# A w_down product by seven block products, woven between those of gate and up

## What is computed

```
xn    = rms_norm(x, norm1)
proj  = xn @ w_in                                  # hyena x0, x1, v | q | k | v
mixed = concat(rms_norm(hyena(proj), hy_gain), rms_norm(window_attention(proj), at_gain))
h     = x + mixed @ w_out
gu    = rms_norm(h, norm2) @ w_gate_up             # 1024 -> 2 * 2816
gate, up = split(gu, 2)
y     = h + (silu(gate) * up) @ w_down             # 2816 -> 1024
```

## Time and profile before

| | us |
|---|---|
| median of 3 runs | 2817.58 (2816.18 to 2820.11) |
| the profiled execution | 2818.18 |
| its span, first to last instruction | 2816.4 |
| TensorE busy in the span | 2738.5 |
| VectorE / ScalarE / GpSimd busy | 1895.5 / 1226.2 / 1028.5 |
| w_down's matmuls, sum of listed durations | 938.7 (2376 of 512 columns) |
| mean granted TensorE clock | 0.991 |

### The profile page before, as it was taken

One profiled execution on the slowest core, in us unless ns is written; L12 is line 12 of the kernel. 1 busy time (PEld: TensorE's weight loads), 2 busy tenths in 40 slices (PEclk: granted clock), 3 DMA queues, 4 the chain that ended last, 5 costly groups with the idle time before them and its releaser, 6 DMA issues.

```text
span 2816.4 us, 38299 instructions
## 1 busy us (share of the span) xinstructions
PE 2738.5 (97%) x14266; PEld 2474.7 (88%) x14266; DVE 1895.5 (67%) x2612; ACT 1226.2 (44%) x1937; POOL 1028.5 (37%) x887
## 2 busy tenths in 40 slices
PE   8989999999998999999999999999999999999999
PEld 6877889888887888878999999999999989999998
DVE  6765676777577787767666666766665676566665
ACT  5564554444547777764232322422223333232321
POOL 1122121233212444464354543334454434343422
PEclk9999999999999999999999999999999999999999
DMA  6476997876897354454223221623322262222221
GB/s 218 146 260 197 300 257 231 282 211 183 230 256 204 111 150 131 121 164 142 86 87 94 86 87 59 244 65 98 94 89 91 72 221 81 65 72 65 71 70 66
DMA packets 388480, 405.30 MB, mean 144 GB/s; under 512 B 46270, under 2 KB 323390, under 8 KB 388007
## 3 DMA queue, kind: packets, MB, share of 16 engines
q1 hardware_dynamic: 358728, 322.50, 39.1%
q0 software_dynamic: 29568, 80.36, 8.9%
HBM read 292.14 MB, written 110.64 MB: 143 GB/s over the span
## 4 chain that ended last, share of the span: by engine, by line
PE 88%; DVE 4%; DMA 3%; ACT 2%; issue 2%; POOL 0%; SPq 0%; DVEq 0%; ACTq 0%; POOLq 0%
PE ff_banks L85 11%; PE ff_banks L87 11%; PE ff_banks L86 11%; PE ff_down L85 7%; PE ff_down L86 7%; PE ff_down L87 7%; PE pr_acc L85 4%; PE pr_acc L86 4%; PE pr_acc L87 4%; PE pr_gen L85 3%; PE pr_gen L87 3%; PE pr_gen L86 3%; PE am_mix L85 2%; PE am_mix L87 2%; PE am_mix L86 2%
## 5 line engine op out<-in xcount | busy, mean ns | idle before, releaser
L2802 POOL TENSOR_TENSOR ff_alo_raw<-ff_alo_raw,ff_silu 128x384 f32<-128x384 f32 x132 | 196.4, 1488 | 698.0 <-DVE ff_alo_raw L3025 624.4
L3047 DVE TENSOR_TENSOR ff_h<-ff_h,ff_down 128x512 f32<-128x512 f32 x396 | 265.1, 685 | 160.5 <-PE ff_down L87 157.4
L85 PE MATMUL ff_banks<-ff_xhi,ff_ghi 128*128 128x384 f32 x924 | 313.4, 339 | 6.3 <-DVE ff_glo L3035 3.8
L85 PE MATMUL ff_down<-ff_dhi,ff_ahi 128*128 128x512 f32 x792 | 313.0, 395 | 3.5 <-issue 3.5
L85 PE MATMUL pr_acc<-pr_xhi,pr_whi 128*128 128x386 f32 (+1 forms) x864 | 303.5, 351 | 11.4 <-DVE pr_xlo L1478 11.4
L86 PE MATMUL ff_down<-ff_dlo,ff_ahi 128*128 128x512 f32 x792 | 313.0, 395 | 0.0
L87 PE MATMUL ff_down<-ff_dhi,ff_alo 128*128 128x512 f32 x792 | 312.7, 395 | 0.0
L87 PE MATMUL ff_banks<-ff_xhi,ff_glo 128*128 128x384 f32 x924 | 312.1, 338 | 0.0
L86 PE MATMUL ff_banks<-ff_xlo,ff_uhi 128*128 128x384 f32 x924 | 311.0, 337 | 0.0
L85 PE MATMUL ff_banks<-ff_xhi,ff_uhi 128*128 128x384 f32 x924 | 310.7, 336 | 0.0
L86 PE MATMUL ff_banks<-ff_xlo,ff_ghi 128*128 128x384 f32 x924 | 310.5, 336 | 0.0
(11 more groups left out here) (308 smaller groups left out, 6518.5 us busy)
## 6 DMA issues: line engine op xcount, KB each, us to landing
ff_glo_raw<-w_gate_up SPq DMA_DIRECT2D x132, 256.0 KB, 3.2
ff_ulo_raw<-w_gate_up SPq DMA_DIRECT2D x132, 256.0 KB
ff_dlo_raw<-w_down SPq DMA_DIRECT2D x66, 512.0 KB, 4.4
pr_raw<-w_in SPq DMA_DIRECT2D x108, 256.0 KB, 6.5
f_dram<-fi_out POOLq DMA_DIRECT2D x32, 512.0 KB, 3.9
fs_a<-f_dram SPq DMA_DIRECT2D x32, 512.0 KB, 9.6
pr_xs<-x SPq DMA_DIRECT2D x18, 512.0 KB, 6.2
xkeep_dram<-pr_xs SPq DMA_DIRECT2D x18, 512.0 KB, 4.6
```

Of the source, the lines that this page charges most:

```text
L85: pe.matmul(out, still[0], moving[0], start=start, stop=False)
L2802: pool.tensor_tensor(block(prod, c), block(prod, c), silu[c][:], ALU.mult).then_inc(tempered, 1)
L3047: dve.tensor_tensor(h[j][:, o], h[j][:, o], down(v), ALU.add).then_inc(added, 1)
```

## The change

**In front.** Rows of w_down are loaded as 44 sets of four blocks of 128x128, one set for each of the first 44 events; GpSimd makes the four sums (or differences) of each set in four subtractions of 128 columns, and SP stores them to `dsum_dram`. Runs of 512 bytes, 256 KB in and 256 KB out for each set.

**In swiglu.** The product with w_down is made from seven block products as well: the activations of the step as 2x2 blocks (2 feature halves by 2 halves of 3 token tiles) with four sums made by GpSimd (`act_sums`), against w_down's blocks or their stored sums. Block product k is 3 triples (`lower(q, k)`), one for each token tile, 512 columns, and is added to its corner of h by three additions (`add(q, k)`). Some products accumulate on what an earlier one left in the bank, after it was read.

Gate and up: two PSUM banks X and Y in place of four. A chain stays open in its bank and is read between its products: ScalarE copies X after products 0, 2 and 4 (`keep`), VectorE adds Y to such a copy for C11, C12, C22, and C21 is read straight from X, by ScalarE's silu for gate and by VectorE's multiplication for up (`corner_straight`). So a product waits until the bank that it adds to was read.

The low and high parts of activations and w_down are made for each block product (`down_high`, `down_low`: 512 columns of w_down, then 384 of activations). The seven `lower(q - 1, k)` stand between the products of step q. The order on ScalarE, VectorE, GpSimd and SP is new. At a turn of group the low parts of T4 and B22 go to GpSimd. The rows h are loaded and the results stored by corners.

```diff
+        def bring_blocks(m):
+            if not 0 <= m < TP:
+                return
+            if m >= TB:
+                sp.wait_ge(t_out[(m - TB) % 2], 16 * ((m - TB) // 2 + 1))
+            n, o = m // 4, m % 4 * P
+            for i in range(2):
+                src = w_down[:, 2 * n + i, :].rearrange("p (h c) -> p h c", h=2)[:, :, o:o + P]
+                sp.dma_start(blocks[:, m % TB, 2 * i:2 * i + 2], src).then_inc(t_in[m % 2], 16)
+
+        def store_blocks(m):
+            if not 0 <= m < TP:
+                return
+            n, o = m // 4, m % 4 * P
+            sp.wait_ge(t_summed, 4 * m + 4)
+            sp.dma_start(dsum_dram[:, :, n, o:o + P].rearrange("x p c -> p x c"), blocks[:, m % TB]).then_inc(t_out[m % 2], 16)
+
         def second_half(rd, i, c):
...
+        def sum_blocks(m):
+            if not 0 <= m < TP:
+                return
+            b11, b12, b21, b22 = (blocks[:, m % TB, k] for k in range(4))
+            pool.wait_ge(t_in[m % 2], 32 * (m // 2 + 1))
+            pool.tensor_tensor(b11, b12, b11, ALU.subtract).then_inc(t_summed, 1)
+            pool.wait_ge(t_summed, 4 * m + 1)
+            pool.tensor_tensor(b12, b22, b12, ALU.subtract).then_inc(t_summed, 1)
+            pool.wait_ge(t_summed, 4 * m + 2)
+            pool.tensor_tensor(b22, b22, b11, ALU.subtract).then_inc(t_summed, 1)
+            pool.wait_ge(t_summed, 4 * m + 3)
+            pool.tensor_tensor(b21, b21, b22, ALU.subtract).then_inc(t_summed, 1)
+
         def evict(rd, i, c):
...
+    HT = WT // 2
     A11, A12, A22, S3, S1, S2, S4 = range(7)
     B11, B21, B22, T3, T1, T2, T4 = range(7)
-    STEPS = ((0, A11, B11), (1, S1, T1), (2, S2, T2), (3, A12, B21), (0, S3, T3), (2, A22, T4), (3, S4, B22))
+    X, Y = 0, 1
+    STEPS = ((X, A11, B11), (Y, A12, B21), (X, S2, T2), (Y, S1, T1), (X, S3, T3), (X, A22, T4), (Y, S4, B22))
...
+
+    NK = 7
+    STILL = (A11, A12, S2, S1, S3, A22, S4)
+    ADDED_TO = (C11, C11, C12, C22, C22, C21, C12)
+    LAST_ADDED = {C11: 1, C22: 4, C21: 5, C12: 6}
+    RAW_DOWN = {0: (0, 0), 1: (1, 0), 6: (1, 1)}
+    SUM_DOWN = {2: 3, 3: 0, 4: 1, 5: 2}
+    BEFORE_ON = {0: 5 - NK, 1: 6 - NK, 2: 0, 3: 1, 4: 2, 5: 4, 6: 3}
...
+        def bring_d(q, k):
...
+            if n >= DR:
+                sp.wait_ge(lowered, n - DR + 1)
+            f = 2 * (q % NC)
+            if k in RAW_DOWN:
+                row, half = RAW_DOWN[k]
+                src = w_down[:, f + row, 512 * half:512 * half + 512]
+            else:
+                src = dsum_dram[SUM_DOWN[k], :, q % NC, :]
+            sp.dma_start(din[n % DR][:], src).then_inc(d_in[n % DR], 16)
+
...
+        def act_sums(q, part):
...
+                pool.tensor_tensor(acts[:, S1], acts[:, S3], acts[:, A22], ALU.add).then_inc(a_summed, 1)
...
+                pool.tensor_tensor(acts[:, S2], acts[:, S1], acts[:, A11], ALU.subtract).then_inc(a_summed, 1)
...
+                pool.tensor_tensor(acts[:, S3], acts[:, A11], acts[:, S3], ALU.subtract).then_inc(a_summed, 1)
...
+                pool.tensor_tensor(acts[:, S4], acts[:, A12], acts[:, S2], ALU.subtract).then_inc(a_summed, 1)
...
                 if q:
+                    temper(q - 1, C12)
+                    act_sums(q - 1, 0)
                     sums(2 * q + 1)
...
+        def product(s, at):
...
+            if at == 0:
+                pe.wait_ge(w_low, 2 * s + 1)
+                if s % 2:
+                    pe.wait_ge(bent, 4 * q + 1 + TURN[C21])
+                elif s:
+                    pe.wait_ge(straight, q)
+            if at == 1 and s:
+                pe.wait_ge(combined, after(s - 1, C12))
+            if at == 2:
+                pe.wait_ge(w_low, 2 * s + 2)
+            if at in (2, 4, 5):
+                pe.wait_ge(copied, 3 * s + {2: 1, 4: 2, 5: 3}[at])
+            if at == 3:
+                pe.wait_ge(combined, after(s, C11))
+            if at == 6:
+                pe.wait_ge(combined, after(s, C22))
...
+        def lower(q, k):
...
+            pe.wait_ge(d_low, n + 1)
+            pe.wait_ge(a_low, n + 1)
+            for j in range(NT):
+                at_least(pe, added, 3 * step_of(q, BEFORE_ON[k]) + j + 1)
+                tok = slice(j * P, (j + 1) * P)
+                last = triple(pe, lowered_in(k, j), (ahi[n % AR][:, tok], alo[n % AR][:, tok]), (dhi[n % DR][:], dlo[n % DR][:]), k in OPENS, True, k not in OPENS)
+            last.then_inc(lowered, 1)
...
             for q in range(NQ):
+                s = 2 * q
+                product(s, 0)
+                product(s, 1)
                 if q == 1:
                     pe.wait_ge(mix_added, 4 * NTT)
                     pe.wait_ge(x_kept, 2 * NTT)
+                lower(q - 1, 0)
+                product(s, 2)
+                product(s, 3)
+                lower(q - 1, 1)
+                product(s, 4)
+                lower(q - 1, 2)
+                product(s, 5)
+                product(s, 6)
+                if q == 0:
+                    close(0)
+                product(s + 1, 0)
+                lower(q - 1, 3)
+                product(s + 1, 1)
+                product(s + 1, 2)
+                lower(q - 1, 4)
+                product(s + 1, 3)
+                product(s + 1, 4)
+                lower(q - 1, 5)
+                product(s + 1, 5)
+                product(s + 1, 6)
                 if q == 0:
                     close(1)
+                lower(q - 1, 6)
+            for k in range(NK):
+                lower(NQ - 1, k)
...
+        def keep(s, n):
+            act.wait_ge(multiplied, step_done(s, (0, 2, 4)[n]))
             if s:
+                act.wait_ge(combined, after(s - 1, (C11, C12, C22)[n]))
+            act.copy(kept[n][:], bank(X)).then_inc(copied, 1)
...
+            if c == C21:
+                act.wait_ge(multiplied, step_done(2 * q, 5))
+                if q:
+                    act.wait_ge(straight, q)
+                act.activation(silu[c][:], bank(X), ACT.Silu).then_inc(bent, 1)
...
+        def down_high(q, k):
...
+            act.copy(dhi[n % DR][:], din[n % DR][:]).then_inc(d_high, 1)
...
+                act.wait_ge(lowered, n - AR + 1)
+            act.copy(ahi[n % AR][:], acts[:, STILL[k]]).then_inc(a_high, 1)
...
+                keep(s, 0)
...
+                keep(s, 1)
+                down_high(q - 1, 2)
+                if turned(q):
+                    row_high(g, T4)
+                    row_high(g, B22)
+                weight_high(s + 1, 0)
+                keep(s, 2)
+                weight_high(s + 1, 1)
+                bend(q, C22)
+                down_high(q - 1, 3)
+                bend(q, C21)
+                bend(q, C12)
...
+                keep(s + 1, 0)
+                down_high(q - 1, 4)
+                weight_high(s + 2, 0)
+                keep(s + 1, 1)
+                down_high(q - 1, 5)
+                if turning(q):
+                    row_high(g + 1, B11)
+                keep(s + 1, 2)
+                if turning(q):
+                    row_high(g + 1, B21)
+                weight_high(s + 2, 1)
+                down_high(q - 1, 6)
+                if turning(q):
+                    row_high(g + 1, T2)
+                down_high(q, 0)
...
+        def corner_straight(q):
+            dve.wait_ge(multiplied, step_done(2 * q + 1, 5))
+            dve.wait_ge(bent, 4 * q + 1 + TURN[C21])
+            if q:
+                dve.wait_ge(a_summed, 4 * q)
+                dve.wait_ge(a_low, step_of(q - 1, 1) + 1)
+            dve.tensor_tensor(acts[:, HELD[C21]], silu[C21][:], bank(X), ALU.mult).then_inc(straight, 1)
...
+        def down_low(q, k):
...
+            n = step_of(q, k)
+            dve.wait_ge(d_high, n + 1)
+            dve.tensor_tensor(dlo[n % DR][:], din[n % DR][:], dhi[n % DR][:].bitcast(F32), ALU.subtract).then_inc(d_low, 1)
+            dve.wait_ge(a_high, n + 1)
+            dve.tensor_tensor(alo[n % AR][:], acts[:, STILL[k]], ahi[n % AR][:].bitcast(F32), ALU.subtract).then_inc(a_low, 1)
...
+        def add(q, k):
...
+            if n:
+                dve.wait_ge(added, 3 * n)
+            for j in range(NT):
+                to = h[NT * half + j][:, o]
+                dve.tensor_tensor(to, to, lowered_in(k, j), ALU.add).then_inc(added, 1)
...
+                add(q - 2, 6)
+                down_low(q - 1, 1)
+                corner(s, C11)
+                if q == 0:
+                    for x in (T4, B22):
+                        row_low(0, x)
+                if turned(q):
+                    row_low(g, T3)
+                add(q - 1, 0)
+                down_low(q - 1, 2)
+                if q:
                     weight_low(s + 1, 0)
+                add(q - 1, 1)
+                if q:
                     weight_low(s + 1, 1)
+                corner(s, C22)
+                if q == 0:
+                    weight_low(1, 0)
+                    weight_low(1, 1)
+                down_low(q - 1, 3)
+                add(q - 1, 2)
+                corner(s, C12)
```

(22 more changed lines are left out.)

579 lines of the change are left out of this document (257 added, 322 removed).

## The result

The kernel with the change takes 2855.7 us (median of 4 runs, 2850.1 to 2856.9), the kernel before 2817.2 us beside it: a ratio of 1.013, 95% interval 1.011 to 1.015. It is slower by 1.3%. The forecast was 2815 us with a range of 2793 to 2845, so the time lies above the range. The profiled execution has a span of 2853.5 us, 37.1 more than before.

What follows compares the result with a forecast made beforehand. TensorE, busy 97% of the span, was taken as the bound. Removed block products -69.3, tail +5, stalls +39 and +12, row pieces +3, opening +2, turns +1, front +4: -3 from 2818.2, so 2815 us; range 2793 to 2845.

Steps and rivals of the forecast that it cites:

- Stall one: Gate's product P6 waits for C22, behind up's weight cast and VectorE's subtraction: 1.2 us in each of 32 steps, +39 us.
- Stall two: Next step's first gate product waits for up's C21 multiplication, behind VectorE's queued work: 0.4 us in 31 steps, +12 us.
- The 0.25 us for steps with row pieces: In 12 steps that also build pieces of the next rows, GpSimd's last sums fall beside a VectorE subtraction: +3 us.
- The tail: From the last product to the last addition: 18.9 us before, 23.9 us after, limited by VectorE, +5 us.
- The front: Bringing, summing and storing 44 w_down blocks in the first 48 events, up to about 430 us: taken as +4 us.
- The rival with a chance of 0.15: In front, 307 GB/s is a transfer ceiling: +11 us over the 4 taken, 2826 to 2832 us; chance 0.15.
- a unit in hand: In front, row and weight loads behind SP's added transfers have one unit, two events, to spare.
- The opening: Start of SwiGLU: B21 is wanted by the second product, not the fourth, up to 4.2 us new idle; +2 us net.
- the gap of 2.07 us: At the opening, the fifth product's existing wait of 2.07 us for ScalarE, said to fall away with the change.
- The turns: Two changes of token group: row parts of 1.7 us lose 3.2 us in each, against 2.9 now; +1 us.
- contention: Rival: GpSimd's work slows VectorE's low parts by 0.8 us in 31 steps, +25 us, 2840 us; chance 0.13.
- clock: Rival: gaps growing from 1.1 to 2 us bring half clock, 2.5 us more in 32 steps, 2895 us; chance 0.04.

Runs made afterwards that it cites:

- all_fixes: Kernel with the change, two VectorE operations moved ahead of subtractions, SwiGLU opening reordered, at turns T4 and B22 low parts on VectorE, C12 and C11 earlier: 2789.6 us, ratio 0.989.

## Why the prediction was wrong

**Right.** Stall one: 1.2 us a step forecast, a gap of 1.00 us released by C22, 1.30 us back when it was taken away. Stall two: 0.4, gaps of 0.27 to 0.35, 0.55 back. Steps of 45.7 us forecast, 45.67 measured. The 512-column low part took 0.68 us alone, as I had interpolated; VectorE's step was 37.2 us where the sum had 35. The 0.25 us for steps with row pieces is not there: steps with and without them take 45.61 to 45.71 us. The tail:

```profile
2824.47 0.39 PE L85 MATMUL ff_banks<-ff_dhi,ff_ahi 128*128 128x512 f32 x1
...
2847.79 1.88 DVE L3223 TENSOR_TENSOR ff_h<-ff_h,ff_banks 128x512 f32<-128x512 f32 x3 [0.32 <-PE ff_banks L87]
```

L6, the first block after the last product, begins at 2824.47, the last addition ends at 2849.67: 25.2 us, where I had 23.9, so 1.3 short. Contention on ordinary steps existed (the low parts of 512 columns average 0.93 us, up to 1.67 beside GpSimd) but fell where nothing waited, as argued.

**The front, 19 us.** The failing step is "I take +4, nearest to the second row, since it shows TensorE itself". That row (760 to 800 us, share 1.16, 277 GB/s) was from another stretch with other transfers; the row for the stretch in question (276 GB/s at a share of 0.97) said that little was left, and the rival worked out from it gave 15 us. Measured between the same landmarks, 18 us: 10.7 idle and 7.3 at half clock, which no term of the front had. The rival with a chance of 0.15 came near the size (its 2826 to 2832 has the stalls, the turns and the opening as forecast), but in part by luck: it has no half clock, and its reason, 307 GB/s as a ceiling, does not hold as it stands, for the kernel before moves 329 over 302 to 342 us. What is shown is that the added transfers cost 20 us; whether by their bytes or by SP's waits for them stays open. I also said that the waits of SP and GpSimd had a unit in hand; SP waited 20 us for set stores, and moving the waits cost up to 81 us.

**The opening, 8 us.** "Up to two products, 4.2 us" for B21 was sized right (4.6), but booked at +2 net, by crediting the gap of 2.07 us. It came to 3: 2.5 of idle and 0.5 of half clock (2.2 lost for 1.7 before). The expectations put 3.4 us on that half clock; but the 6.8 us at 0.50 began 2.4 us before TensorE resumed, so only half of 4.5 us is lost. What was missed is L0 in step 1. That SP's loads of w_down go at least 7 us ahead of their cast was worked out for an ordinary step. At the opening the first load stood behind a store that waited for VectorE:

```profile
1339.04 0.37 SPq L1953 DMA_DIRECT2D xt_dram<-am_xt  x1
1339.58 1.65 SPq L2770 DMA_DIRECT2D ff_dlo_raw<-w_down  x2
1343.32 0.62 ACT L3090 CAST ff_dhi<-ff_dlo_raw 128x512 fp32r<-128x512 f32 x1 [8.87 <-DMA ff_dlo_raw<-w_down]
```

That is 5.2 us of idle and 1.5 at half clock, which had no term, and nearly all of the 8 us.

**The turns, 13 us.** "3.2 us lost in each" added row parts of 1.7 us to two chains. Two steps failed in it. It did not sum VectorE's work over the turn: twice 37.2 us and five row parts of 1.7 are 83 us, before any contention, in two steps of 88, and with T4 and B22 (all_fixes) it was busy for 36.00 of 36 us. And it left GpSimd's two row parts out of the contention, although and the page's rule stood in the same text. I had asked it of stall two only, where it did not bite; at the turn it did, and brought half clock with it. That was the rival "contention" in another place, and the rival "clock" with a smaller price.

The direction was open in the forecast (0.35 for slower). The size was missed because each rival was held against the forecast alone, while something near three of them came at once.
